# Gated-DeltaNet decay differences: from a DRAM round trip to matmuls and PSUM

## The reference

```python
gam = jnp.cumsum(gc, axis=1)
diff = gam_h[:, :, :, None] - gam_h[:, :, None, :]
dec_incl = jnp.exp(jnp.where(incl, diff, -jnp.inf))
a_mat = jnp.einsum('blhk,bshk->bhls', kb, kc) * dec_strict
t_mat = triangular_solve(eye + a_mat, eye)
qk = jnp.einsum('blhk,bshk->bhls', qc, kc) * dec_incl
o = qk @ v_new + (qc * jnp.exp(gam)) @ S
```

## Time and profile before

| what | value |
|---|---|
| median of 3 runs | 1339.87 us |
| the profiled execution's own time | 1341.55 us |
| its span, first to last instruction | 1339.9 us |
| PE busy | 1237.2 us (92%) |
| PE weight load busy | 1104.4 us (82%) |
| DVE busy | 618.3 us (46%) |
| ACT busy | 468.8 us (35%) |
| POOL busy | 440.6 us (33%) |
| mean granted TensorE clock | 0.93 |
| chain that ended last, by engine | PE 73%, DVE 15%, ACT 4%, issue 3%, DMA 2%, POOL 2% |

### The profile page before, as it was taken

One profiled execution on the slowest core, in us unless ns is written; L12 is line 12 of the kernel. 1 busy time (PEld: TensorE's weight loads), 2 busy tenths in 40 slices (PEclk: granted clock), 3 DMA queues, 4 the chain that ended last, 5 costly groups with the idle time before them and its releaser, 6 DMA issues.

```text
span 1339.9 us, 26257 instructions
## 1 busy us (share of the span) xinstructions
PE 1237.2 (92%) x10744; PEld 1104.4 (82%) x10744; DVE 618.3 (46%) x1089; ACT 468.8 (35%) x779; POOL 440.6 (33%) x372
## 2 busy tenths in 40 slices
PE   6999999889968867899999989998999999999999
PEld 5999987756746446887798965797999999999998
DVE  4699645235378466711427435339443333410003
ACT  6324144155323504432455234355222222222222
POOL 6434432233303501054233320061343444343330
PEclk8999999879958957898699989998999999999999
DMA  5332430255516930233422385240322332323311
GB/s 138 95 79 64 111 97 7 73 164 171 178 52 200 282 121 2 66 110 96 127 65 79 89 251 181 93 142 2 101 87 82 93 95 80 91 81 89 89 46 68
DMA packets 193169, 138.57 MB, mean 103 GB/s; under 512 B 16023, under 2 KB 185416, under 8 KB 193050
## 3 DMA queue, kind: packets, MB, share of 16 engines
q1 hardware_dynamic: 183394, 115.46, 29.3%
q0 software_dynamic: 7200, 20.23, 4.9%
q10 hardware_dynamic: 2456, 1.21, 0.3%
HBM read 128.89 MB, written 7.97 MB: 102 GB/s over the span
## 4 chain that ended last, share of the span: by engine, by line
PE 73%; DVE 15%; ACT 4%; issue 3%; DMA 2%; POOL 2%; POOLq 0%; SPq 0%; DVEq 0%; ACTq 0%
PE PS L259 66%; PE PS L262 7%; DVE PROJ L1837 3%; DVE SC L665 2%; DVE PROJ L1838 1%; DVE PROJ L665 1%; DVE XT L665 1%; DVE XN L893 1%; POOL W_LO L243 1%; DVE XN_parts L884 1%; DVE XN L665 1%; DVE RSQ L891 1%; DMA PROJ<-in_x_sample 1%; ACT PROJ L1240 0%; ACT W_HI L234 0%
## 5 line engine op out<-in xcount | busy, mean ns | idle before, releaser
L243 POOL TENSOR_TENSOR W_LO<-W,W_HI 128x1024 fp32r<-128x1024 f32 (+1 forms) x130 | 314.9, 2425 | 666.1 <-ACT W_HI L234 665.9
L259 PE MATMUL PS<-XN_parts,W_HI 128*128 128x272 f32 x1184 | 340.6, 288 | 0.0
L259 PE MATMUL PS<-OM_parts,W_HI 128*128 128x272 f32 x960 | 277.0, 288 | 0.0
L259 PE MATMUL PS<-SC_parts,W_HI 128*128 128x272 f32 (+2 forms) x832 | 244.4, 294 | 3.3 <-POOL W_LO L243 3.0
L259 PE MATMUL PS<-SC_parts,W_LO 128*128 128x272 f32 (+2 forms) x832 | 241.2, 290 | 0.0
L259 PEld LDWEIGHTS PS<-XN_parts,W_HI 128*128 128x128 f32 x1184 | 223.1, 188 | 0.0
L259 PE MATMUL PS<-OM_parts,W_LO 128*128 128x272 f32 x704 | 203.9, 290 | 0.0
L234 ACT ACTIVATE W_HI<-W 128x1024 fp32r<-128x1024 f32 (+1 forms) x130 | 134.9, 1041 | 196.9 <-PE PS L259 196.9
L259 PEld LDWEIGHTS PS<-OM_parts,W_HI 128*128 128x128 f32 x960 | 181.3, 189 | 0.1
L259 PEld LDWEIGHTS PS<-SC_parts,W_HI 128*128 128x128 f32 x832 | 157.4, 189 | 8.0 <-issue 5.6
L259 PEld LDWEIGHTS PS<-SC_parts,W_LO 128*128 128x128 f32 x832 | 157.0, 189 | 0.0
(11 more groups left out here) (385 smaller groups left out, 2166.2 us busy)
## 6 DMA issues: line engine op xcount, KB each, us to landing
W<-in_w_gu SPq DMA_DIRECT2D x44, 512.0 KB, 3.8
W<-in_w_in SPq DMA_DIRECT2D x30, 512.0 KB, 3.8
W_scratch<-in_cache_moba_k SPq DMA_DIRECT2D x64, 128.0 KB, 2.5
W_scratch<-in_cache_moba_k POOLq DMA_DIRECT2D x64, 128.0 KB, 2.6
W_scratch<-in_cache_moba_v SPq DMA_DIRECT2D x64, 128.0 KB, 3.7
W_scratch<-in_cache_moba_v POOLq DMA_DIRECT2D x64, 128.0 KB, 3.7
W<-in_w_xkv SPq DMA_DIRECT2D x16, 512.0 KB, 3.7
W<-in_w_down SPq DMA_DIRECT2D x16, 512.0 KB, 4.0
```

The costliest lines, as they stand in the source:

```text
L243: nc.gpsimd.tensor_tensor(hi_lo(n)[1], raw_chunk(n), hi_lo(n)[0].bitcast(F32), ALU.subtract).then_inc(S("weights_split"), 1)
L259: return nc.tensor.matmul(out, lhsT, rhs, start=start, stop=stop, skip_group_check=True)
```

## The change

The DRAM tensor, the write to it and all seven reads are removed, with the waits for them. In "gdn", PE now makes for each prompt tile one 4-row matmul with `pairsel` (272 columns, one of the four halves of `g_logd`) ahead of its 8 matmuls, and four one-hot 4-row matmuls (`dec_tensor`) behind them, before `g_mm` is raised; tile 4 gets the one-hot ones only. DVE calls `dec_vector` on the result after waiting for `g_mm`, in place of the four instructions. ACT copies the spread rows from PSUM to `g_logd` after each of the first four exponentials.

```diff
-            sp.wait_ge(S("rows_made"), 1)
-            sp.dma_start(decay_rows, rows[:, 3, :]).then_inc(S("decay_rows_out"), 16)
...
-            spread_decays(0, g_dec[:, 2], P)
-            spread_decays(1, g_dec[:, 3], P)
-            spread_decays(4, g_dec_s[0:NS], NS)
-            for e in range(2):
-                sp.dma_start(g_logd[e * DH:(e + 1) * DH, :, :], ...)
             after(sp, "hgrn")
-            spread_decays(2, g_dec[:, 0], P, "g_spread2")
-            spread_decays(3, g_dec[:, 1], P, "g_spread3")
...
 (gdn_vector)
-                ex = g_decay(i)
-                v.wait_ge(S("g_spread") if i in (0, 1, 4) else S(f"g_spread{i}"), 80 if i in (0, 1, 4) else 16)
+                ex = hl(g_p1[:, i % 4, :], w)
+                v.wait_ge(S("g_mm"), i + 1)
...
-                for h in range(H):
-                    last = V.scalar_tensor_tensor(ex[:, h, :], ex[:, h, :], cumtok[0:w, i, 4 + h:5 + h], msk, ALU.subtract, ALU.add)
-                last.then_inc(S("g_m"), 1)
-                v.wait_ge(S("g_mm"), i + 1)
+                dec_vector(ex, 4 * (i % 2) + 2, 4, i, w).then_inc(S("g_m"), 1)
...
 (gdn_scalar)
                 A.activation(ex, ex, ACT.Exp).then_inc(S("g_exp"), 1)
+                if i < 4:
+                    s.wait_ge(S("rows_spread"), 4 + i + 1)
+                    A.activation(half(g_logd[:, i // 2, :], i % 2), bank(3 + 4 * (i % 2))[:, 0:HT], ACT.Copy).then_inc(S("rows_spread_out"), 1)
...
 (gdn_tensor)
+                if i < 4:
+                    if i >= 2:
+                        pe.wait_ge(S("rows_spread_out"), i - 1)
+                    mm(bank(b_ + 3)[:, 0:HT], pairsel[0:H, i // 2, :], half(rows[:, 3, :], i % 2), True, True)\
+                        .then_inc(S("rows_spread"), 1)
...
-                last.then_inc(S("g_mm"), 1)
+                dec_tensor(pe, b_ + 2, 3, t0, w, w).then_inc(S("g_mm"), 1)
```

More of the change, by code:

```diff
@@ L136, in __call__ @@
                 return v
-        decay_rows = nc.dram_tensor("decay_rows", (H, T), F32).ap()
         proj = PROJ[:, :].rearrange("p (c t) -> p c t", t=T)
@@ L381, in build @@
         t_vm = m(H * NB * DH)
-        g_dec = g_p1.rearrange("p n (h l) -> p n h l", l=P)
-        g_dec_s = carve(SC, 4 * T + 4 * 512, H, NS)
         base = C_Z * T
@@ L419, in cx_slot @@
             return cx_slots[n % 4]
-        H_JOBS = [[(i, P) for i in range(4)] + ([(i, NS) for i in range(2)] if j < 3 else []) for j in range(8)]
-        H_MM = [sum(len(jobs) for jobs in H_JOBS[:j + 1]) for j in range(8)]
-        H_PACKED = 5
         hT = PROJ[:, 0:KF * T].rearrange("p (c t) -> p c t", t=T)
@@ L548, in _ @@
             sp.dma_start(t_s0, a["state_hgrn"][0].rearrange("b (c e) k v -> (e k) b c v", e=2)).then_inc(S("state_in"), 16)
[L549 to L554, removed]
-            spread_decays(0, g_dec[:, 2], P)
-            spread_decays(1, g_dec[:, 3], P)
-            spread_decays(4, g_dec_s[0:NS], NS)
-            for e in range(2):
-                sp.dma_start(g_logd[e * DH:(e + 1) * DH, :, :],
-                             decay_rows.rearrange("(o c e) t -> e o c t", o=1, e=2)[e].to_broadcast((DH, 2, T))).then_inc(S("g_spread"), 16)
             after(sp, "hgrn")
-            spread_decays(2, g_dec[:, 0], P, "g_spread2")
-            spread_decays(3, g_dec[:, 1], P, "g_spread3")
             for i in range(2):
@@ L2353, in gate_vector @@
                 link(last)
+        H_JOBS = [[(i, P) for i in range(4)] + ([(i, NS) for i in range(2)] if j < 3 else []) for j in range(8)]
+        H_MM = [sum(len(jobs) for jobs in H_JOBS[:j + 1]) for j in range(8)]
+        H_PACKED = 5
         def h_width(j):
@@ L2499, in build @@
         GB = (slice(0, DH), slice(DH, P))
-        def g_decay(i):
-            return g_dec[:, (i + 2) % 4] if i < 4 else g_dec_s[0:NS]
         g_unit = lev[:, 7, 0:DH]
@@ L2539, in gdn_vector @@
             for i, (t0, w, _) in enumerate(TILES):
-                ex = g_decay(i)
-                v.wait_ge(S("g_spread") if i in (0, 1, 4) else S(f"g_spread{i}"), 80 if i in (0, 1, 4) else 16)
+                ex = hl(g_p1[:, i % 4, :], w)
+                v.wait_ge(S("g_mm"), i + 1)
                 if i == 4:
                     v.wait_ge(S("g_al_free"), 1)
-                msk = (negmask if w == P else negmask_s)[0:w, 0:w]
-                for h in range(H):
-                    last = V.scalar_tensor_tensor(ex[:, h, :], ex[:, h, :], cumtok[0:w, i, 4 + h:5 + h], msk, ALU.subtract, ALU.add)
-                last.then_inc(S("g_m"), 1)
-                v.wait_ge(S("g_mm"), i + 1)
+                dec_vector(ex, 4 * (i % 2) + 2, 4, i, w).then_inc(S("g_m"), 1)
                 v.wait_ge(S("g_exp"), i + 1)
@@ L2626, in gdn_scalar @@
                 s.wait_ge(S("g_m"), i + 1)
-                ex = g_decay(i)
+                ex = hl(g_p1[:, i % 4, :], w)
                 A.activation(ex, ex, ACT.Exp).then_inc(S("g_exp"), 1)
-            s.wait_ge(S("g_spread"), 80)
+                if i < 4:
+                    s.wait_ge(S("rows_spread"), 4 + i + 1)
+                    A.activation(half(g_logd[:, i // 2, :], i % 2), bank(3 + 4 * (i % 2))[:, 0:HT], ACT.Copy).then_inc(S("rows_spread_out"), 1)
+            s.wait_ge(S("rows_spread_out"), 4)
             hgrn_norm_scalar(s, 0)
@@ L2664, in gdn_tensor @@
                         c0 = (2 * m_ + h // 2) * w
-                        last = mm(bank(b_ + h % 2)[0:w, c0:c0 + w], gk[r, h // 2, sl], rhs[r, h // 2, sl], True, True)
-                last.then_inc(S("g_mm"), 1)
+                        mm(bank(b_ + h % 2)[0:w, c0:c0 + w], gk[r, h // 2, sl], rhs[r, h // 2, sl], True, True)
+                dec_tensor(pe, b_ + 2, 3, t0, w, w).then_inc(S("g_mm"), 1)
                 if i == 3:
@@ L2669, in gdn_tensor @@
             pe.wait_ge(S("g_mats"), 4)
+            pe.wait_ge(S("rows_spread_out"), 4)
             hgrn_norm_tensor(pe)
```

## The result

The changed kernel takes 1350.1 us (median of 4 runs, 1344.37 to 1350.89), the kernel before 1340.41 (4 runs in the same job, 1336.91 to 1341.55): ratio 1.0069, 95% interval 1.0043 to 1.0095. It is slower, as forecast, but by 9.7 us where the sum said 4.5, and outside the range. The profiled execution took 1350.26 us (span 1348.6), and two more on record took 1348.55 and 1350.59. A second comparison, with more runs, gave the change 1349.77 (12 runs, 1345.41 to 1355.98) against 1342.28 (35 runs, 1336.74 to 1352.65): ratio 1.0053, interval 1.0028 to 1.0079.

What follows compares the result with a forecast made beforehand. PE bounds the kernel overall (92% busy), but in "gdn" the chain runs through DVE and ACT. Tile 0 +3.7, DVE +1.0 and page wait -0.2 made +4.5: 1344.4 us from a median of 1339.87, range 1339.5 to 1348.2.

Steps and rivals of the forecast that it cites:

- a wait for PE at tile 2 or 3: Sign that would show the prediction wrong: DVE waiting for PE at these later tiles of "gdn"; no size given.
- The sign of a shorter stage before "gdn": Sign of being wrong: the stage ahead of "gdn" shorter by more than half a microsecond.
- The first rival: In "gdn", the clock comes up by 490.5 us and no loss is visible: 1341.8 to 1343.7 us, chance 0.27.
- The second: Rival: PE bounds the tile loop at 5.6 instead of 4.7 us per tile: +6.5, 1346.4 us, chance 0.17.
- The term of tile 0: Start of "gdn": PE's longer first tile raises `g_mm` later, so DVE's differences start 3.7 us later.
- My end of 4.2: Upper bound in us for tile 0's delay, with each four-row record 15% dearer next to 64-row ones.
- The cover at tile 3: Tile 3 ready on PE at 506.8, wanted by DVE at 507.3: PE's work stays hidden by 0.5 us.
- DVE's own term: Tiles 0 to 3: two `dec_vector` instructions take longer than the four old ones, +1.03 us, all on the chain.
- On the median of the runs, 1339.87: Base of the forecast: this median, 1.7 us below the profiled execution's 1341.55, giving 1344.4.
- Everything from there on follows in the same order: From the norm to the end, each step is released by the one before, so +4.5 us passes on.
- The page wait, -0.22: Before "gdn": without the five reads, PE's 0.41 us wait for a page of values goes, gaining 0.22 us.
- the rival of the exposed transfers: The removed transfers, 1.0 MB or 3.4 us, were not hidden: net +1.3, 1341.2 us, chance 0.07.

Runs made afterwards that it cites:

- pair_last: Changed kernel with the `pairsel` matmul moved behind the one-hot matmuls in every tile: 1347.06 us (one run).
- rows128: Changed kernel with the same `pairsel` and one-hot matmuls over all 128 rows, on query values in place of the decays: 1348.23 us (one run).
- delay: Kernel before with DVE's first square of "gdn" issued five times instead of once: +4.7 us against the kernel before, ratio 1.0038.
- delay_long: Kernel before with eight extra squares on DVE ahead of tile 0's differences: +10.7 us against the kernel before, ratio 1.0087.
- decfirst: Changed kernel with the one-hot matmuls first under their own semaphore, `pairsel` last: +2.0 us (0 to 3.9) against the kernel before.
- decfirst_stt: As decfirst, with the old four DVE instructions per tile reading the decays from PSUM: +1.5 us against the kernel before, ratio 1.0006.
- pipe_before: Kernel before with the next tile's differences ahead of this tile's products on DVE: 1341.77 against 1343.49 us, ratio 0.9987.
- pipe_again: The same reordered kernel as pipe_before, timed again: 1340.63 against 1342.17 us for the kernel before, ratio 0.9983.

## Why the prediction was wrong

- **The mechanism** was right: DVE waits for tile 0's `g_mm`, no wait at tiles 1 and 2, DVE's two instructions at 0.69, ACT and the transfers of the loop at 0, the low clock across tile 0. But one of my signs of being wrong came, "a wait for PE at tile 2 or 3", of 0.18 us. The sign of a shorter stage before "gdn" can't be judged: the kernel before alone differs by 6.4 us up to there. The first rival doesn't stand, as the clock did not come up. The second, PE at 5.6 a tile, came at about half its price: 5.44 in tiles 0 and 3, which adds 0.54 at tile 0 and 0.27 at tile 3 where it had 0.9 and 0.4.
- **The term of tile 0 was mis-sized**: "The new tile 0 at 1.2 GHz: two records of `pairsel` 1.00, own matmuls 1.87, eight one-hot records 2.07, together 4.94", a delay of 3.7. It measured 5.44 and 4.23. Prices per record left out 0.20 for `pairsel` behind an idle PE (1.20, shown by pair_last) and 0.30 at the change from the own matmuls to the one-hot ones. rows128 has the same two numbers with 128 rows (483.12 to 484.33, and 2.17 from there to 486.50), so it is not four rows that cost it. What does is open. My end of 4.2 is about this value, but for another reason, so that is luck.
- **The cover at tile 3** was "by 0.5 us only", with 4.7 us for PE's part of a tile. PE needed 5.44 there, 0.74 more, which turns a cover of 0.5 into a wait of about 0.24; it cost 0.27. DVE's own term was +0.85, not +1.03. Together 4.23 + 0.85 + 0.27 = 5.35, which is the loop's +5.33, where 4.7 was forecast.
- **"On the median of the runs, 1339.87, ... which I forecast from"** is the step that did most to put the time outside the range. Three runs don't fix this kernel, and they are three of the four that the result compares with: over the 69 of the three later jobs its mean is 1343.3, 3.4 above my base, and it ranges from 1336.7 to 1353.4. From 1343.3, my own +4.5 gives 1347.8, and the range would have ended at 1351.6; with the measured loop, +5.3, it gives 1348.6. The second comparison's mean was 1350.1, with an uncertainty of some 2 us. Whether the first job's lower times are chance or its chip is not known, as the record names the chips of the later jobs alone.
- **"Everything from there on follows in the same order"** holds on average. The differences measured against the loops: delay +4.7 for +5.31, delay_long +10.7 for +10.61, decfirst +2.0 for +1.97, decfirst_stt +1.5 for +1.60, pipe_before and pipe_again -2.0 for -2.84, the change +6.6 for +5.33. Each loop value lies within its interval. In a single pair of executions it does not hold: the trace after carries 2.3 + 1.2 us behind the loop that the second execution of the same kernel lacks.
- **The page wait, -0.22**, "Bounds 0 to -0.41", was mis-sized, since I took one execution for its price: over eight with the reads it is 0 to -2.5, -0.6 on average. Here the rival of the exposed transfers has a part in it. Its price was wrong too: the pages give 138.57 MB before and 136.93 after, so 1.6 MB are gone and not 1.0, which at its 300 GB/s is some 5.5 us in place of 3.4.

Of the 9.7 us, then, 5.3 are the loop, shown by delay and by taking the parts away. Behind it, the step from the norm's start to DVE's first instruction on its results goes by how the clock stands, as in these rows of DVE (before, then after):

```profile
511.55 0.42 DVE L665 TENSOR_TENSOR PROJ<-CN,PS 128x256 f32<-128x256 f32 x1 [1.59 <-PE PS L259]
...
515.79 0.42 DVE L643 TENSOR_TENSOR PROJ<-CN,PS 128x256 f32<-128x256 f32 x1 [2.32 <-PE PS L258]
```

The step is 4.56, 4.65 and 5.06 us in three executions of before, at a mean granted clock of 0.60, 0.58 and 0.52, and 5.09 and 4.56 in two of the changed kernel, at 0.50 and 0.60: 0.1 more on average. The page gives back about 0.6. That makes some 4.8 expected, and 6.6 +- 2.2 was measured where there are most runs. No run shows the rest of the 9.7 to belong to the change: it comes from 4 runs each, against a base that was 3.5 us below the mean of the later jobs. A steady part of 1 or 2 us can't be excluded.

"TensorE: Matmul & The Clock Gate" of the Trainium skill (the row of its terms on the time spent throttled) puts the price of a low clock at the throttled time times one minus the clock's share, here half. Within the span the granted clock was at its low level for 187.7 us in the first execution of before and 167.3 in the second, which by that rule is 10.2 us (an estimate). The spans differ by 4.7 (1339.9 and 1335.2), less than half of it. PE waits for others in part of the time at the low clock, as in the loop here, which would make the rule an upper end; no run separates that.

## What to carry to other kernels

A hidden read costs little (here some 0.6 us for seven). Replacing it by work on an engine that "is idle anyway" costs the whole of that work on the first tile, where nothing has been made ahead. Put what the next engine wants first at the head of the producer's list, and only then the rest. Read a producer's price from start to start across kinds of instruction, not as a sum of durations. Before forecasting from a median, look at how far the runs of that kernel spread, compare executions only in the stretch that was edited, and read a short wait for a transfer in several of them.

## What the runs showed of the hardware

- With four-row matmuls among tile 0's, PE was busy for 11.5 us without a break and the granted clock stayed at 0.50 (low in the loop in 6 executions of 6); with 128-row ones of the same count, on other values, it rose 3.8 us after the start (1 execution).
- At 1.2 GHz two `pairsel` records behind an idle PE took 1.20 us, 0.20 over their 0.50 each, and the own matmuls in front of the one-hot ones took 2.17, 0.30 over their 1.87. With 128 rows the same two steps took 1.21 and 2.17.
- `scalar_tensor_tensor` of 128x128 from PSUM takes as long as from SBUF, 1.13 us for four.
- PE's wait for one page was 0 to 2.25 us in 8 executions with five reads issued beside its load, and 0 in the 6 without them.
- The same kernel spreads over 16.6 us (1336.7 to 1353.4 in 69 runs), 1.2%, on one core.
